# Identity turns in the pauses of the opening, a last block finished by pieces, and three weight rows loaded straight to their places

## The reference, cut to what matters

```python
def trunk_layer(x, p, ...):
    h = rms_norm(x, g_pre_mix)
    cb, cc, ch, q, k, v, ga, gb = jnp.split(h @ w_in, IN_SPLITS, axis=-1)
    ...
    merged = jax.nn.sigmoid(ga) * y_a + jax.nn.sigmoid(gb) * y_b
    x = x + rms_norm(merged @ w_o, g_post_mix)
    ...
    x = x + rms_norm((jax.nn.gelu(gate) * val) @ w_down, g_post_ffn)
    e = (p @ w_ple) * jax.nn.sigmoid(rms_norm(x, g_ple_gate) @ w_ple_gate)
    x = x + rms_norm(e, g_post_ple)
```

## Time and profile before

| what | value |
|---|---|
| median of 3 runs | 1815.45 us (1812.14 to 1816.53) |
| the profiled execution's own time | 1811.77 us |
| its span, first to last instruction | 1810.0 us |
| PE busy | 1786.1 us, 99% of the span |
| DVE busy | 1030.1 us, 57% |
| ACT busy | 587.0 us, 32% |
| HBM read and written | 108.57 MB and 27.18 MB, 75 GB/s over the span |

### The profile page before, as it was taken

One profiled execution on the slowest core, in us unless ns is written; L12 is line 12 of the kernel. 1 busy time (PEld: TensorE's weight loads), 2 busy tenths in 40 slices (PEclk: granted clock), 3 DMA queues, 4 the chain that ended last, 5 costly groups with the idle time before them and its releaser, 6 DMA issues.

```text
span 1810.0 us, 29936 instructions
## 1 busy us (share of the span) xinstructions
PE 1786.1 (99%) x10820; PEld 1688.4 (93%) x10820; DVE 1030.1 (57%) x1934; ACT 587.0 (32%) x1030; POOL 38.3 (2%) x34
## 2 busy tenths in 40 slices
PE   7999999999999999999999999999999999999997
PEld 6989998999899899988899999999999999999885
DVE  6255145325524546656676756666666667576564
ACT  6335244334523452244311111111111111125664
POOL 1000000000000000000100000000000000004100
PEclk9999999999999999999999999999999999999999
DMA  4312221231122124354111111111111111143342
GB/s 160 99 51 64 85 68 49 65 101 47 62 83 68 45 96 152 108 187 135 60 49 42 48 48 47 38 46 47 48 36 47 48 46 48 37 138 103 104 135 93
DMA packets 160062, 137.07 MB, mean 76 GB/s; under 512 B 11838, under 2 KB 140186, under 8 KB 159962
## 3 DMA queue, kind: packets, MB, share of 16 engines
q1 hardware_dynamic: 149018, 130.89, 23.1%
q10 hardware_dynamic: 10944, 4.90, 1.0%
HBM read 108.57 MB, written 27.18 MB: 75 GB/s over the span
## 4 chain that ended last, share of the span: by engine, by line
PE 97%; DMA 1%; DVE 1%; ACT 1%; issue 0%; ACTq 0%; SPq 0%; DVEq 0%
PE pair L1909 16%; PE pair L1907 16%; PE pair L1908 16%; PE pair L2264 11%; PE pair L1978 10%; PE pair L1980 9%; PE pair L1979 9%; PE pair L1932 5%; PE pair L2117 2%; PE pair L2146 2%; PE pair L2047 1%; DMA raw<-in_w_o 1%; PE pair L2340 0%; PE pair L2168 0%; PE pair L2342 0%; PE pair L2341 0%
## 5 line engine op out<-in xcount | busy, mean ns | idle before, releaser
L1978 PE MATMUL pair<-xh,wh 128*128 128x384 f32 (+1 forms) x952 | 335.1, 352 | 0.2
L1907 PE MATMUL pair<-bh,wh 128*128 128x384 f32 (+1 forms) x1008 | 330.1, 327 | 0.0
L1909 PE MATMUL pair<-bh,wl 128*128 128x384 f32 (+1 forms) x1008 | 328.8, 326 | 0.0
L1908 PE MATMUL pair<-bl,wh 128*128 128x384 f32 (+1 forms) x1008 | 328.4, 326 | 0.0
L1980 PE MATMUL pair<-xh,wl 128*128 128x384 f32 (+1 forms) x952 | 311.5, 327 | 0.0
L1979 PE MATMUL pair<-xl,wh 128*128 128x384 f32 (+1 forms) x952 | 311.0, 327 | 0.0
L1327 DVE TENSOR_TENSOR wl<-raw,wh 128x1024 fp32r<-128x1024 f32 x112 | 137.0, 1223 | 128.4 <-ACT wh L813 128.1
L1978 PEld LDWEIGHTS pair<-xh,wh 128*128 128x128 f32 x952 | 179.1, 188 | 14.4 <-issue 10.8
L1907 PEld LDWEIGHTS pair<-bh,wh 128*128 128x128 f32 x1008 | 189.2, 188 | 0.4
L1908 PEld LDWEIGHTS pair<-bl,wh 128*128 128x128 f32 x1008 | 189.3, 188 | 0.0
L1909 PEld LDWEIGHTS pair<-bh,wl 128*128 128x128 f32 x1008 | 189.2, 188 | 0.0
(11 more groups left out here) (252 smaller groups left out, 2652.6 us busy)
## 6 DMA issues: line engine op xcount, KB each, us to landing
raw<-in_w_up SPq DMA_DIRECT2D x88, 256.0 KB, 3.2
raw<-in_w_in SPq DMA_DIRECT2D x80, 256.0 KB, 3.2
raw<-in_w_down SPq DMA_DIRECT2D x44, 256.0 KB, 2.7
gat<-gate_spill SPq DMA_DIRECT2D x16, 544.0 KB, 4.4
x_spill<-x SPq DMA_DIRECT2D x16, 512.0 KB, 3.0
gate_spill<-stg SPq DMA_DIRECT2D x32, 192.0 KB, 1.9
xn<-in_x_prompt SPq DMA_DIRECT2D x8, 512.0 KB, 7.8
pk<-in_cache_k SPq DMA_DIRECT2D x64, 64.0 KB, 1.9
```

The source lines that it names most:

```text
L1907: t_.matmul(b, h, xhi, start=(i == 0), stop=False)
L1908: t_.matmul(b, h, xlo, start=False, stop=False)
L1909: ins = t_.matmul(b, l, xhi, start=False, stop=(i == n - 1))
L1978: t_.matmul(b, h, xhi, start=(k == 0), stop=False, skip_group_check=True)
```

## The change

Five things are edited.

1. PE turns the identity against itself into a spare bank (idle) at four places of the opening: 42 times before x0_turn(0), 18 times before x0_turn(1), 11 times before the first unit, 11 times after x0_turn(2). The results are not read.
2. The opening has a new order: weight tile 0 is loaded ahead of x block 2; ACT does whi and x0_high(0) before block 2's square, and root(3, 3) after the second whi; the first unit takes block 0 alone and then blocks 1 and 2 in one pass of 256 columns; the turns of blocks 3, 4 and 5 come before parts 1, 3 and 5 of in_tile(1, 0).
3. Weight rows 5, 6 and 7 of w_o are loaded in one transfer each to the place where their rest will lie (woraw), ahead of rows 3 and 4, as soon as the branches are done.
4. The gate's sums move to pairs[2 - b % 2], the other sum to pairs[0], and block 0's gate product waits for all but the last four of the down units' additions.
5. The last block's gate product is made in two halves of 512 features and its other product in pieces of 512, 256 and 256; ACT and DVE work by these pieces, the gain is multiplied in before the root is known, and the result is stored in two halves.

```diff
+WARM = (42, 18, 11, 11)
...
+DIRECT = 5
+woraw = {k: at(f"wor{k}", [P, D], R1 + (k - 1) * 8192 + 4096) for k in range(DIRECT, KD)}
...
+def gate_pair(b):
+    return pairs[2 - b % 2]
+ple_pair = pairs[0]
+PIECE = [(0, 512), (512, 768), (768, 1024)]
+def ple_piece(i):
+    return (ple_pair[0:NS, 0:512], ple_pair[0:NS, 512:768], gate_pair(BLK - 1)[0:NS, 0:256])[i]
...
     x_start(0)
     broadcast(g_mix, "g_pre_mix", g_mix_in)
     x_start(1)
+    load(in_job(0, 0))
     x_start(2)
-    load(in_job(0, 0))
     x_start(3)
...
     hold(p_unit, ENDS[J_OUT - 1])
+    for k in range(DIRECT, KD):
+        sp.dma_start(woraw[k][:, :], w_o[:, k:k + 1, :].rearrange("p o n -> p (o n)")).then_inc(wo_in[k], 16)
     hold(d_mrg, 8 * NG)
     load(row(w_o, 3))
-    for k in range(4, 7):
-        load(row(w_o, k))
+    load(row(w_o, 4))
+    job.step(KD - DIRECT)
     broadcast(g_out, "g_post_mix", g_in[0])
-    load(row(w_o, 7))
     up_rows(0, None)
     x_block(0)
...
-    for b in range(NBK):
+    for b in range(BLK):
         if b + 2 < NBK:
             x2_block(b + 2)
         hold(d_out, b + 1)
-        rows_ = block_rows(b)
-        sp.dma_start(natural(b, yp_o, ys_o), e_[b % 2][0:rows_, :]).then_inc(y_out[b % 2], 16)
-        if b + 1 < NBK:
-            x2_again(b + 1)
-    hold(y_out[0], 16 * 5)
+        sp.dma_start(yp_o[:, b, :], e_[b % 2][:, :]).then_inc(y_out[b % 2], 16)
+        x2_again(b + 1)
+    for h in range(2):
+        hold(d_out, NBK + h)
+        sp.dma_start(ys_o[:, 512 * h:512 * h + 512], e_[0][0:NS, 512 * h:512 * h + 512]).then_inc(y_out[0], 16)
...
     x0_root(1, 1)
+    whi()
+    x0_high(0)
     x0_square(2)
     x0_root(2, 1)
-    whi()
-    x0_high(0)
-    x0_square(3)
     x0_high(1)
-    x0_square(4)
-    x0_square(5)
-    x0_root(3, 3)
+    for b in range(3, 6):
+        x0_square(b)
     x0_high(2)
     whi()
-    for b in range(6, NBK):
-        x0_square(b)
-    x0_root(6, 3)
+    x0_root(3, 3)
+    x0_square(6)
+    x0_square(7)
     stn = [Count() for _ in range(NG)]
...
+            q_high(0)
+            x0_square(8)
             x0_high(3)
-            q_high(0)
+            x0_root(6, 3)
             x0_high(4)
             x0_high(5)
...
-    for k in range(1, KD):
+    for k in range(1, DIRECT):
         whi_to(wout[k][0], ENDS[J_OUT])
+    for k in range(DIRECT, KD):
+        act.wait_ge(wo_in[k], 16)
+        s_.activation(wout[k][0][:, :], woraw[k][:, :], ACT.Copy).then_inc(a_hi, 1)
...
         if b + 2 < NBK:
             y_second(b + 2)
-    e_squares(NBK - 1)
+    def last_block():
+        e, gate = e_[0][0:NS, :], gate_pair(BLK)[0:NS, :]
+        tables("sigmoid_and_others")
+        act.wait_ge(d_rz, NBK)
+        act.wait_ge(y_out[0], 16 * (BLK // 2))
+        for h in range(2):
+            act.wait_ge(p_g, NBK + h)
+            cols = slice(512 * h, 512 * h + 512)
+            s_.activation(e[:, cols], gate[:, cols], ACT.Sigmoid,
+                          scale=st[0:NS, 45 + N_Z + BLK:46 + N_Z + BLK]).then_inc(a_gate, 1)
+        tables("natural_log_exp_and_others")
+        for i, (c0, c1) in enumerate(PIECE):
+            act.wait_ge(d_e, NBK + i)
+            s_.activation(junk2[0:NS, c0:c1], e[:, c0:c1], ACT.Square, accum_out=st[0:NS, 101 + i:102 + i]).then_inc(a_sum, 1)
+        act.wait_ge(a_sum, 3)
+        act.wait_ge(d_sum, 2)
+        r = st[0:NS, 45 + N_E + BLK:46 + N_E + BLK]
+        then(s_.activation(r, st[0:NS, 103:104], ACT.Ln, scale=1.0 / D, bias=st[0:NS, 105:106]))
+        s_.activation(r, r, ACT.Exp, scale=-0.5).then_inc(a_ne, 1)
+    last_block()
...
     v.memset(st[:, 100:101], EPS).then_inc(d_eps, 1)
-    for k in range(1, KD):
+    for k in range(1, DIRECT):
         wlo_to(*wout[k])
+    for k in range(DIRECT, KD):
+        dve.wait_ge(a_hi, job.step())
+        v.tensor_tensor(wout[k][1][:, :], woraw[k][:, :], f(wout[k][0][:, :]), ALU.subtract).then_inc(d_lo, 1)
...
+        first_sum, both_sums, m, t = (st[0:NS, i:i + 1] for i in (104, 105, 110, 111))
+        r = scale_of(N_E + BLK, NS)
+        def piece(i):
+            c0, c1 = PIECE[i]
+            dve.wait_ge(a_gate, NBK + (1 if i else 0))
+            dve.wait_ge(p_ple, NBK + i)
+            v.tensor_tensor(e[:, c0:c1], e[:, c0:c1], ple_piece(i), ALU.mult).then_inc(d_e, 1)
+        def gained(c0, c1, pieces):
+            dve.wait_ge(d_e, BLK + pieces)
+            v.tensor_tensor(times_gain[:, c0:c1], e[:, c0:c1], g_ple[0:NS, c0:c1], ALU.mult).then_inc(d_ne, 1)
+        dve.wait_ge(d_x2, NBK)
+        piece(0)
+        gained(0, 512, 1)
+        piece(1)
+        dve.wait_ge(a_sum, 1)
+        v.tensor_scalar(first_sum, st[0:NS, 101:102], 1.0 / D, EPS, ALU.mult, ALU.add).then_inc(d_sum, 1)
+        piece(2)
+        dve.wait_ge(a_sum, 2)
+        dve.wait_ge(d_sum, 1)
+        v.tensor_scalar(both_sums, st[0:NS, 102:103], 1.0 / D, first_sum, ALU.mult, ALU.add).then_inc(d_sum, 1)
+        gained(512, 1024, 3)
+        dve.wait_ge(a_sum, 3)
+        dve.wait_ge(d_sum, 2)
+        then(v.tensor_scalar(m, st[0:NS, 103:104], 1.0 / D, both_sums, ALU.mult, ALU.add))
+        dve.wait_ge(a_ne, NBK)
+        then(v.tensor_scalar(t, r, r, m, ALU.mult, ALU.mult))
+        then(v.tensor_scalar(t, t, -0.5, 1.5, ALU.mult, ALU.add))
+        then(v.tensor_scalar(r, t, r, None, ALU.mult))
+        dve.wait_ge(x3_in, 16 * NBK)
+        dve.wait_ge(d_ne, BLK + 2)
+        for h in range(2):
+            cols = slice(512 * h, 512 * h + 512)
+            v.scalar_tensor_tensor(out=e[:, cols], in0=times_gain[:, cols], scalar=r, in1=x3[0:NS, cols],
+                                   op0=ALU.mult, op1=ALU.add).then_inc(d_out, 1)
+    product(BLK - 1)
+    finish(BLK - 1)
+    last_block()
 @block.tensor
...
+        def idle(i):
+            for _ in range(WARM[i]):
+                turned(banks[1][:, 0:P], ident[:, :])
         def by_blocks():
             b = open_unit(0, 0)
-            for i in range(3):
-                if i == 1:
+            for at_, end in ((0, P), (P, 3 * P)):
+                if at_:
                     x0_turn(2)
-                pe.wait_ge(d_x0l, 2 * (i + 1))
-                o = b[:, i * P:(i + 1) * P]
+                    idle(3)
+                pe.wait_ge(d_x0l, 2 * (end // P))
+                o, cols = b[:, at_:end], slice(at_, end)
                 for k in range(KD):
-                    (h, l), xhi, xlo = tall(0, k), xh[:, k, span(i)], xl[:, k, span(i)]
+                    (h, l), xhi, xlo = tall(0, k), xh[:, k, cols], xl[:, k, cols]
                     t_.matmul(o, h, xhi, start=(k == 0), stop=False, skip_group_check=True)
                     t_.matmul(o, h, xlo, start=False, stop=False, skip_group_check=True)
...
         if first:
+            idle(0)
             x0_turn(0)
+            idle(1)
             x0_turn(1)
+            idle(2)
             begin_job()
             by_blocks()
             begin_job()
-            in_tile(1, 0, {5: [(x0_turn, 3)], 7: [(x0_turn, 4)]})
-            x0_turn(5)
+            in_tile(1, 0, {1: [(x0_turn, 3)], 3: [(x0_turn, 4)], 5: [(x0_turn, 5)]})
             pe.wait_ge(d_x0l, 12)
             conv_rows()
             in_tile(0, 1, {6: [(x0_turn, 6)]})
             past(0)
-            in_tile(1, 1, {1: [(x0_turn, 7)], 4: [(x0_turn, 8)]})
+            in_tile(1, 1, {1: [(x0_turn, 7)], 3: [(x0_turn, 8)]})
             pe.wait_ge(d_x0l, 2 * NBK)
             past(1)
...
     def gate_rows(b, k):
-        ins = rows_by(pairs[b % 2], b, k, x2h, x2l, lambda t, c: wgate[k][t][:, 512 * c:512 * c + 512], k == 0, k == KD - 1)
+        ins = rows_by(gate_pair(b), b, k, x2h, x2l, lambda t, c: wgate[k][t][:, 512 * c:512 * c + 512], k == 0, k == KD - 1)
         if k == KD - 1:
...
     X2_AT, Y_AT = [3, 4, 3, 3] + [2] * 5, [6, 7, 7, 7] + [6] * 5
-    pe.wait_ge(d_unit, WIDE1)
-    for b in range(NBK):
+    def cols_by(o, k, hi, lo, w, first, last):
+        h, l = hi[:, k, span(BLK)], lo[:, k, span(BLK)]
+        t_.matmul(o, h, w(0), start=first, stop=False, skip_group_check=True)
+        t_.matmul(o, h, w(1), start=False, stop=False, skip_group_check=True)
+        return t_.matmul(o, l, w(0), start=False, stop=last, skip_group_check=True)
+    def last_block():
+        pe.wait_ge(a_gate, BLK - 1)
+        pe.wait_ge(d_xl, 2 * NBK)
+        for c0 in (0, 512):
+            for k in range(KD):
+                ins = cols_by(gate_pair(BLK)[0:NS, c0:c0 + 512], k, x2h, x2l, lambda t: wgate[k][t][:, c0:c0 + 512], k == 0, k == KD - 1)
+            ins.then_inc(p_g, 1)
+        pe.wait_ge(d_e, BLK)
+        pe.wait_ge(a_gate, BLK)
+        for i, (c0, c1) in enumerate(PIECE):
+            for k in range(2):
+                o = k * 512 + c0 % 512
+                ins = cols_by(ple_piece(i), k, ph, pl, lambda t: (wh, wl)[t][c0 // 512][:, o:o + c1 - c0], k == 0, k == 1)
+            ins.then_inc(p_ple, 1)
+    pe.wait_ge(d_unit, WIDE1 - 4)
+    for b in range(BLK):
+        if b == 1:
+            pe.wait_ge(d_unit, WIDE1)
         if b >= 2:
```

(36 more changed lines are left out.)

## The result

The kernel after takes 1801.32 us (median of 4 runs, 1801.23 to 1801.74), the kernel before 1815.99 us on the same chip (4 runs, 1812.14 to 1816.76). The ratio is 0.9924, 95% interval 0.9907 to 0.9941: faster by 14.7 us in the medians. The forecast was 1806.4 us, 9.0 us less, in a range from 1800 to 1812.5.

What follows compares the result with a forecast made beforehand. PE, 97% of the chain, was taken as the bound, with gains only at its waits, slow stretches or tail. 5.8 + 0.6 + 0.6 + 2.0 = 9.0 us off the median 1815.45 gave 1806.4 us, range 1800 to 1812.5.

Steps and rivals of the forecast that it cites:

- The opening: Start of the kernel up to conv_rows: new order and identity turns bring conv_rows from 35.98 to 30.1, counted as 5.8 us less.
- the walk: Opening's new order stepped through with the old profile's durations: clock up at 9.0 us, conv_rows at 30.1.
- Turns don't raise the clock: Rival, opening: identity turns leave PE's clock low; no change (1815.3 us) or slower (1819.7 us); chance 0.17.
- The clock rises later: Rival, opening: run-up ends only at 12.4 or 15.4 us, total gain 6 to 7.7 us, 1808 to 1809.5; chance 0.15.
- Block 6 late: Opening, behind conv_rows: block 6 scaled about 33.3, up to 0.3 us back; within third rival, chance 0.15 shared with the fourth.
- Row 3 late: Fourth rival, output product: weight row 3 late behind three direct rows, +0.5 for -0.6, 1807.5 us; chance 0.15 shared with third.
- the last of the sum: Whole kernel: profiled execution lies 3.7 us under the median, so the forecast against median 1815.45 is 1806.4 us.
- The output product: Output product, weight row 7: direct loads of rows 5 to 7 remove PE's wait, 0.6 us less.
- The gate product's start: Ahead of the first gate matmul: PE's wait for the last addition goes, 0.6 us less, not given back.
- The last block: Kernel's end: work in pieces saves 2.3 us behind the last matmul, costs PE 0.3, so 2.0 us less (0.5 to 2.8).

## Why the prediction was right, and where its sizes were off

**The opening.** Forecast 5.8 us, measured 6.0 between the two profiled executions. conv_rows was put at 30.1 and stood at 29.96, x0_low(2) at 19.7 and the wide pass began at 19.90, block 3 scaled at 23.3 and turned at 23.40. Two guesses inside it erred. The clock rose near 5.5 us and not at 9.0; this had no effect, since PE waits for scaled blocks and rests on both sides of it, as the walk had it. The wide pass took 0.12 us a matmul and not 0.14, 3.0 us in place of 3.4; this had one, since PE has no wait from 19.90 to conv_rows. But the pass began 0.2 later than walked, which takes back half of it: that conv_rows came within 0.14 us is luck to that extent. The new order and the turns don't simply add up: the turns alone bring conv_rows to 33.60 (2.4 of the 6.0), the new order alone, in the profile without turns, to 34.59 (1.4), both to 29.96.

**The rivals of the clock.** "Turns don't raise the clock" fell in the first 7 us: 42 turns of the identity alone raised it. The Trainium skill, page "TensorE: Matmul & The Clock Gate", section "Part 4: PE-mode transpose", says of one kernel that the upper level doesn't engage for transposes; here it did, and the measurement decides. "The clock rises later" didn't occur either in any profile of the kernel after. "Block 6 late" didn't occur: PE had no wait of note behind conv_rows. "Row 3 late" didn't occur: its high part begins at 767.30, 8.9 us behind the first output matmul, where it was 7.6 to 9.4 with the old loads, and PE doesn't wait for it.

**The median.** The step that failed is the last of the sum: "That execution lies 3.7 us under the median of the runs, so against the median, 1815.45, the forecast is 1806.4". It took the 3.7 us for something that both kernels share. They were the late clock rise of about half of the executions of the kernel before, 5.2 us in the profile of one, and the change removes it. Against the profiled execution's own time the forecast was 1802.8 and 1801.29 was measured; against the lower group of before (about 1811.5) the gain is 10.2 us, against the upper one (about 1816.9) 15.6, and the median of before depends on how many of its runs fall in each. The spread of 4.4 us stood in the times before; I used it for the range and didn't ask what made it. That 1801.3 lies in the range is partly luck: its lower end, 1800, was put there partly for that spread, and the kernel after has hardly any (0.5 us).

**The output product.** Forecast 0.6. In the pair of profiles it is 0.8, but the run without the direct loads shows 0.0 in the median, and 24.57 us from the first output matmul to the turn of fr where the kernel after has 24.54: I had read a wait of one execution as one of the kernel. The four other profiles with the old loads have no such wait. The direct loads can be left out at no cost that these runs show.

**The gate product's start.** Forecast 0.6, measured 0.7 between profiles and 0.9 by undoing it (0.7 in its profile, without the 0.1 that was there at conv_rows).

**The last block.** Forecast 2.0, measured 3.0 between profiles and 3.3 by undoing it (3.0 behind the last matmul). From the last sum to the last addition it took 4.23 us, forecast 4.2. The rest was mis-sized: the twelve 256-column matmuls cost PE nothing extra (1.37 us for what I put at 1.7, a pitch of 0.114), and the store in halves ends 2.8 us behind the last addition instead of 3.4, which I had left out. Before, from the last matmul's end to the last addition was 6.6.

## What to carry to other kernels

When a kernel's times fall into groups, find the place where an execution of each group differs before pricing a change: a part that does nothing in one profile may be worth microseconds in the median. While an engine's clock depends on its work, a pause is not free on it even if nothing waits: cheap work in every pause keeps the following stretch fast, and one pause left empty can undo all that was filled before it. A wait that one profile shows at the edge of a transfer's arrival should be checked in a second profile before it is counted. When two parts of a change act on the same stretch, as the new order and the turns do, their prices have to be measured together and apart.

## What the runs showed of the hardware

The moment at which PE's clock rises is not fixed by the work ahead of it. The same 42 identity turns, begun at 1.6 us with nothing before them, take 6.34 us in one profile (of the kernel after with the first turns only) and 7.66 in another (of the kernel before with the turns):

```profile
1.60 6.34 PE L2027 MATMUL pair<-ident 128*128 128x128 f32 x42 [1.60 <-POOL ident L764]
```

```profile
1.60 7.66 PE L1934 MATMUL pair<-ident 128*128 128x128 f32 x42 [1.60 <-POOL ident L743]
```

By the two pitches, as an estimate, some 14 or 15 of them were slow in the first and some 27 in the second. So the rise came after 3.1 us in the one and 5.8 in the other. It came after 3.9 us in the profile of after, 4.5 us where the turns began with the second group, and 3.4 us behind the fall at the wide pass, but also after 7.4, 12 and 20 us where the work began with separate turns and waits, and after 17 us behind the fall near 11.6. What sets the long ones stays open; no run here isolates it. Pauses of 2.26 and 1.87 us were each followed by a fall in the profiles; a pause of 1.67 us in some executions only: in the profile of the kernel before with turns it was, in the two profiles of the kernel before (1.67 and 1.66 us ahead of conv_rows) it wasn't.

A matmul of 256 columns costs PE nearly what one of 128 does: 0.120 and 0.112 us at the upper level, 0.213 and 0.215 at the lower (here each with a new stationary operand). That is why the 24 matmuls of one pass over two blocks took 3.0 us, where the 48 of two single-block passes take 5.4 at the upper level.

The granted clock column reads 1.00 from 0 us to the first rise although the pitch is that of the lower level; after a fall it reads 0.50 correctly. The experiments point to no version better than the kernel after.
